# One core, three fused blocks: fixed places for the linear attention's products, an earlier load of the input, and a last column block that is gated and stored by pairs

## The chip, the cores and the metric

The kernel runs on one core of a Trainium2 chip. The metric is the device time of one execution in microseconds (us), and the time of a kernel is the median of its runs. TensorE is written PE here, as in the profile (PEld is its weight load), VectorE DVE, ScalarE ACT, GpSimd POOL, and SyncE, which issues most loads, SP.

## The reference, cut to what matters

Three blocks follow one another on an input of 1024 positions by 1024 features, all in float32. The change touches the first half of block one and the last step of block three.

Block one, first half:

```
h = rmsnorm(x) * norm_mix_g
z = h @ w_in                      # q, k, v, g, a_f, a_b, su, sv
o_f = gla(q, k, v, log_a_f), o_b = the same from right to left, strict
  per chunk of 64 positions: b = cumsum(log_a)
  scores = (q exp(b - b_mid)) @ (k exp(b_mid - b))^T, masked
  state  = exp(b_last) * state + (k exp(b_last - b))^T @ v
  o      = scores @ v + (q exp(b)) @ state
o_gla = rmsnorm_per_head(o_f + o_b) * silu(g)
o_sgu = gelu(su) * (w_s @ rmsnorm(gelu(sv)) + b_s)
x = x + [o_gla, o_sgu] @ w_out
```

Block three, last step:

```
gate = sigmoid(rms_norm(h) @ w_pg);  pe = p @ w_pp
h = h + gate * pe
out = rms_norm(h) * final_g
```

## The kernel before, in words

Every product with a weight matrix is done in three passes: the weights and the activations are each split into a high and a low float32r part, and high by high, high by low and low by high are added in one bank of PSUM (`three`, `mms`). Weights come in units of 256 columns (one unit is one matrix of 1024 rows by 256 columns, 1 MB; some are smaller). A unit passes through four hands: SP loads it (`sp_unit`, one of 3 raw buffers), ACT makes the high part (`act_unit`, L311, one of 2 buffers, after PE has finished the unit two before), DVE makes the low part by a subtraction (`dve_unit`, L320), and PE multiplies (`pe_unit` waits for both parts). Each engine's program calls its own function once a turn; the first turn handles two units (three for SP), so that ACT and DVE are one unit ahead of PE and SP two.

The order of the work is written out by hand, one program for each engine; the same generator code is run on every engine, so that step s of a round has the same meaning everywhere. Each engine runs its instructions in that order, and semaphores tie them together. A `fence` waits for everything of the stage before.

Start: POOL makes an identity and zeroes four 128 by 128 tiles; SP loads 24 small parameter vectors into them (`sp_setup`) and four lambda vectors; PE transposes the four tiles and DVE copies them to `PC`, whose columns are scales and biases; DVE and ACT work out lambda. Then all engines pass the fence "setup", and SP loads x in 8 tiles of 512 KB. ACT squares a tile and sums it (L484), DVE and POOL make the reciprocal root, DVE scales (L562), PE transposes (L359), ACT and DVE split the transposed tile into high and low (L523, L531). The 1024 positions are handled in two halves of 4 tiles. ACT splits the first two weight units after the first half's transposed tiles (`between`), and DVE does its part there too. Then PE does the product for the gates ("a", half 0), the transposes of half 1, and the product "a" of half 1.

Linear attention (`rounds`): 40 pieces of the projection `z = h @ w_in` are called fills. One fill is 48 products of 256 columns or 24 of 512 columns, some 5.7 us of PE. There are ten units (`FILL`: qk0, v0, v1, qk1, g0, g1, sv0, sv1, su0, su1) of four fills each, here called F0 to F39. The attention has four rounds n (head pair 0 and 1, each in both directions) of 11 steps. In round n `back` does the attention of n and `front` prepares the gates of n+1. On PE: step 0 scores of n (64 small products) and the gates' product of n+1 (`la`); steps 1 to 4 the chunk products `kv`, each in two banks of the ring PB of four; steps 6 to 9 the outputs `go`; step 7 a transpose (`kdT`). On DVE: step 1 masks the scores (L1045), steps 2 to 5 read `kv` and run the state forward (L1058, 15 dependent instructions), step 2 also the cumulative sums of n+1 (L952, L954, L961 or L963, L966), steps 3 and 4 the gated q and k (L973, L978, L979), steps 6 and 7 two more of that kind (L982, L987), steps 7 to 10 read `go`. In round 2, `out` for head pair 0 is added: ACT squares (step 0), DVE the mean (step 1, L582), DVE the scaling (step 2, L593), PE four transposes `goT` (step 3, L359), DVE the gating (step 4, L1100). The fills are spread over the steps by `weave`: 8, 4, 4 and 6 of them over the 11 steps of rounds 0, 1, 2 and 3, which puts them after steps 0, 1, 2, 4, 5, 7, 8, 9 in round 0, after steps 0, 3, 6, 9 in rounds 1 and 2, and after steps 0, 2, 4, 5, 7, 9 in round 3. ACT and DVE handle a new unit at the first fill of the unit before it. The last ten fills stand in the tail after round 3.

End (`pe_final` and its partners): for each of four blocks n of 256 columns, PE does `pg` (gate, unit of 1 MB, four pieces of 48 products), then `pp` (embedding, 256 KB, four pieces); ACT takes the sigmoid of a `pg` piece, DVE multiplies by the `pp` piece (L3782), POOL adds to X3 (L3795). After block 3, ACT squares the 8 tiles (L484), DVE and POOL make the reciprocal roots of each half of 4 tiles (L492, L497), DVE scales the tiles (L1583), and SP stores each tile when it is scaled.

## Time and profile before

| | |
|---|---|
| median of 3 runs | 3949.09 us (3943.42 to 3951.37) |
| the profiled execution's own time | 3947.51 us |
| its span, first to last instruction | 3945.6 us |
| PE busy | 3713.4 us, 94% of the span |
| DVE, ACT, POOL busy | 2167.5, 1653.1, 520.3 us |
| PE's share of the chain that ended last | 78% |
| mean granted TensorE clock | 0.973 |

The span is the traced stretch, and the 1.9 us between it and the execution's own time lie around it. "Granted clock" is the share of full TensorE speed that the chip allowed. A timeline row gives start, duration, engine, line, operation, what is written from what, the count, and in brackets the idle time of that engine before it with what ended it. PE bounds the kernel for most of its length, so a microsecond is worth something where PE stands idle or slow, and at both ends of the span, where PE has nothing to do.

### The profile page before, as it was taken

Reading aid. Unit: us, or ns where it says so; the run is one execution under the profiler, and the core shown is the slowest. Engines: PE = TensorE matmul, PEld = TensorE weight load, DVE = VectorE, ACT = ScalarE, POOL = GpSimd, SP = SyncE. Lnnn points to the kernel's source line nnn. Section 1 sums busy time; section 2 is a strip of 40 time slices with the busy share of each in tenths; the row PEclk is TensorE's granted clock in tenths of the full one; section 3 lists DMA queues with packets and bytes.
Section 4 is the critical chain, followed back from the end, with each engine's and each line's share of the span. In section 5 each row is a group of like instructions: output and inputs, shape, how many; then the busy total and the mean of one; then the engine's idle time right before and its main releaser. Section 6 shows DMA issues by size and latency. Waiting matters only on the chain.

```text
span 3945.6 us, 48879 instructions
## 1 busy us (share of the span) xinstructions
PE 3713.4 (94%) x20470; PEld 3102.4 (79%) x20470; DVE 2167.5 (55%) x2859; ACT 1653.1 (42%) x2267; POOL 520.3 (13%) x437
## 2 busy tenths in 40 slices
PE   6979999999999899989999998989999999989998
PEld 5758988877787677777777777978877778778998
DVE  4343344334446566645665655358888877853332
ACT  4322232121113555646776674144555545542132
POOL 0000010010001243510000000012222221210001
PEclk9989999999999899999999999999999999999999
DMA  3101211111111111010111114121111111143111
GB/s 95 33 11 50 75 59 54 43 51 46 43 54 55 43 33 43 12 49 24 33 35 27 35 48 163 49 75 43 43 43 38 49 48 38 38 183 132 44 44 59
DMA packets 196399, 211.32 MB, mean 54 GB/s; under 512 B 7943, under 2 KB 171732, under 8 KB 196180
## 3 DMA queue, kind: packets, MB, share of 16 engines
q1 hardware_dynamic: 191572, 191.42, 15.3%
q10 hardware_dynamic: 4608, 16.78, 1.1%
q8 instruction: 162, 2.65, 0.3%
q14 instruction: 57, 0.47, 0.0%
HBM read 174.62 MB, written 33.55 MB: 53 GB/s over the span
## 4 chain that ended last, share of the span: by engine, by line
PE 78%; DVE 9%; ACT 6%; issue 4%; DMA 1%; POOL 1%; SPq 0%; DVEq 0%; ACTq 0%; POOLq 0%
PE pd L211 66%; PE pq L211 9%; PE pd L359 2%; PE pq L359 1%; ACT t L311 1%; DVE t L320 1%; DVE t L2989 1%; ACT t L2586 1%; DVE t L3426 1%; ACT t L523 1%; DVE t L2981 0%; DVE t L1923 0%; DVE t L1495 0%; DVE t L3411 0%; DVE t L531 0%
## 5 line engine op out<-in xcount | busy, mean ns | idle before, releaser
L211 PE MATMUL pd<-t 128*128 128x512 f32 (+2 forms) x15920 | 3080.9, 354 | 41.6 <-DVE t L1495 10.1
L211 PEld LDWEIGHTS pd<-t 128*128 128x128 f32 x15920 | 2556.5, 191 | 513.0 <-issue 90.2
L211 PE MATMUL pq<-t 128*128 128x128 f32 (+5 forms) x3222 | 542.8, 331 | 83.6 <-DVE t L3465 21.5
L211 PEld LDWEIGHTS pq<-t 128*128 128x128 f32 (+2 forms) x3222 | 391.6, 182 | 184.4 <-issue 47.3
L311 ACT ACTIVATE t<-t 128x2048 fp32r<-128x2048 f32 (+2 forms) x150 | 244.9, 1633 | 677.9 <-PE pd L211 634.0
L320 DVE TENSOR_TENSOR t<-t 128x2048 fp32r<-128x2048 f32 (+2 forms) x150 | 297.3, 1983 | 287.8 <-ACT t L311 287.4
L1495 DVE TENSOR_TENSOR t<-pd,t 128x512 f32<-128x512 f32 x256 | 171.2, 689 | 115.7 <-PE pd L211 115.7
L1486 DVE TENSOR_TENSOR t<-t 128x512 fp32r<-128x512 f32 x64 | 45.8, 719 | 261.3 <-POOL t L1474 261.3
L3378 POOL TENSOR_TENSOR t<-t 128x512 f32<-128x512 f32 x56 | 89.8, 1603 | 616.8 <-ACT t L3322 608.9
L2989 DVE SCALAR_TENSOR_TENSOR t<-t 128x1024 f32<-128x1024 f32 x120 | 169.6, 1413 | 0.5
L2981 DVE SCALAR_TENSOR_TENSOR t<-t 128x1024 f32<-128x1024 f32 x120 | 166.2, 1385 | 1.7
L2709 DVE COPY t<-pd 128x512 f32<-128x512 f32 x64 | 44.3, 691 | 217.6 <-PE pd L359 217.6
L359 PE MATMUL pd<-t 128*128 128x128 f32 x800 | 119.8, 294 | 42.5 <-DVE t L562 18.6
L359 PEld LDWEIGHTS pd<-t 128*128 128x128 f32 x800 | 101.1, 152 | 65.2 <-issue 20.9
L2586 ACT ACTIVATE t<-t 128x1024 f32<-128x1024 f32 x128 | 145.8, 1142 | 13.8 <-DVE t L2663 13.8
L2658 DVE CUSTOM_DVE_ANT_0 t<-pq,t 128x1024 f32<-128x1024 f32 x128 | 151.2, 1219 | 0.0
L3322 ACT ACTIVATE t<-t 128x1024 f32<-128x1024 f32 x56 | 59.4, 1062 | 215.4 <-DVE t L3413 215.4
L1474 POOL TENSOR_TENSOR t<-t 128x512 f32<-128x512 f32 x64 | 68.2, 1067 | 613.1 <-ACT t L1424 613.1
L1424 ACT ACTIVATE t<-pd 128x512 f32<-128x512 f32 x64 | 38.3, 598 | 244.9 <-PE pd L211 244.9
L3426 DVE COPY_PREDICATED t<-t,pq 128x512 f32<-128x512 int32 x128 | 94.7, 743 | 70.1 <-PE pq L211 69.7
L1591 POOL TENSOR_TENSOR t<-t 128x2 f32<-128x2 f32 x8 | 10.4, 1303 | 917.5 <-DVE t L2826 857.1
L713 DVE TENSOR_TENSOR t<-pd,t 128x512 f32<-128x512 f32 x48 | 33.2, 691 | 176.5 <-PE pd L211 176.5
(295 smaller groups left out, 2830.5 us busy)
## 6 DMA issues: line engine op xcount, KB each, us to landing
t<-in_w_in_dram SPq DMA_DIRECT2D x97, 512.0 KB, 4.3
t<-in_w_mlp_dram SPq DMA_DIRECT2D x32, 1024.0 KB, 5.3
t<-in_w_out_dram SPq DMA_DIRECT2D x20, 1024.0 KB, 5.1
t<-in_w_in_dram SPq DMA_DIRECT2D x16, 1024.0 KB, 5.2
t<-in_x_dram SPq DMA_DIRECT2D x16, 512.0 KB, 6.6
x_scratch<-t SPq DMA_DIRECT2D x16, 512.0 KB, 2.6
ym_scratch<-t SPq DMA_DIRECT2D x16, 512.0 KB, 2.6
t<-x_scratch SPq DMA_DIRECT2D x16, 512.0 KB, 20.0
```

What stands on the lines that cost most here:

```text
L211: ins = e.matmul(out, l, r, start=(first and j == 0), stop=(last and j == n - 1), skip_group_check=True)
L311: e.activation(WH[i % 2][:, 0:z], WR[i % 3][:, 0:z], ACT.Copy).then_inc(*at.inc("wh", "wh", i))
L320: e.tensor_tensor(WL[i % 3][:, 0:z], WR[i % 3][:, 0:z], WH[i % 2][:, 0:z].bitcast(F32), SUB).then_inc(*at.inc("wl", "wl", i))
L359: ins = e.transpose(b[:, j * 128:(j + 1) * 128], s, ident[:, :])
L1474: e.tensor_tensor(q[:, :], r[:, :], r[:, :], MUL).then_inc(*at.inc("pool", "q", j, m, th, free=("r", j, m, th)))
L1495: e.tensor_tensor(X1[:, tt, half(nh)], PD.of("down", j, tt, nh)[:, :], X1[:, tt, half(nh)], ADD).then_inc(*at.inc("dve", "xadd", j, tt, nh ...
L2586: e.activation(s[:, r, :], s[:, r, :], ACT.Exp, bias=x[:, 2 + r:3 + r], accum_out=x[:, 4 + r:5 + r]).then_inc(*at.inc("act", "sexp", n))
L2658: e.tensor_tensor_reduce(out=s[:, r, :], in0=PQt[r][:, :], in1=bias[:, 896 - 128 * tt:896 - 128 * tt + 1024], scale=2.0 ** -(h + 1), scala ...
L2981: e.scalar_tensor_tensor(a[:, :], p[:, k:k + S], taps(k, g), a[:, :], MUL, ADD).then_inc(*at.inc("dve", "ctaps", g))
L2989: e.scalar_tensor_tensor(a[:, :], p[:, k:k + S], taps(k, g), a[:, :], MUL, ADD).then_inc(*at.inc("dve", "ctaps", g))
L3378: e.tensor_tensor(v4(z[:, :], w_)[:, :, 0, :], v4(k[:, :], w_)[:, :, 0, :], v4(dd[:, :], w_)[:, :, 0, :], MUL).then_inc(*at.inc("pool", "h ...
L3426: e.copy_predicated(At[:, th * 4:th * 4 + 4, :], bc(Mi[:, l:l + 1, :], [128, 4, 128]), four(PB.of("lv", h, l, th))).then_inc(*at.inc("dve" ...
```

## The change

Four edits, all in the order of work; no product is added or left out.

1. Start. SP's first instructions are the loads of x tiles 0 to 3, then weight unit 0, then x tiles 4 to 7, then the small vectors of tiles 1 to 3 and the lambda vectors. The ten small vectors of tile 0 are loaded from ACT's own queue. The fence "setup" is gone on all engines. PE transposes only tile 0 before x; the other three, and lambda, come after the product "a" of half 1. X0, XN0 and the parameter tiles have memory of their own, side by side.
2. Weight units one by one: the first turn of each engine handles one unit, and one more call stands in `act_norm`, `dve_norm` and twice in `sp_program`. ACT and DVE split unit 0 between the squares of the two halves.
3. Rounds: the fills have fixed places (`FILLS`), 7, 5, 5 and 5 in rounds 0 to 3; DVE handles the next unit at the third fill of a unit, not at the first (but for qk0); the steps of `out` on DVE and PE move from 1, 2, 3, 4 to 2, 4, 5, 6.
4. End. In block 3, `pp` comes before `pg` and writes into PB; after each `pg` piece ACT takes the sigmoid, DVE multiplies and adds to X3 itself, ACT squares the two tiles of the piece into SBUF, DVE and POOL make their reciprocal roots, and DVE scales them one piece later.

```diff
     def act_unit(e):
-        n = turn("act")
-        for i in ([0, 1] if n == 0 else [n + 1]):
-            if i < len(units):
+        i = turn("act")
+        if i < len(units):
...
+    def act_setup(e):
+        e.wait_ge(*at["PR0", 0])
+        for j, (name, ap) in enumerate(COLS[0]):
+            r = col[name]
+            e.dma(PRc[0][r:r + ap.shape[0], :], ap, "col_in", 0, j)
...
     def pe_setup(e):
         e.wait_ge(*at["const"])
+        PB.put(2, ("col", 0))
+        pe_col(e, 0, PB.of("col", 0))
+
+    def pe_setup_rest(e):
+        for i in range(1, 4):
+            pe_col(e, i, e.take(PB, "col", i))
...
     def act_norm(e, X, v, ready, gname, between=lambda e: None):
-        for th in range(2):
-            act_squares(e, X, v, th, ready)
+        act_squares(e, X, v, 0, ready)
+        between(e)
+        act_squares(e, X, v, 1, ready)
...
             for j in range(4):
                 if late:
                     dve_fill_out(e, *late)
-                if j == 0:
+                if j == (0 if name == "qk0" else 2):
                     dve_unit(e)
...
+    FILLS = [(0, 2, 3, 4, 6, 8, 9), (0, 2, 3, 4, 8), (0, 2, 3, 4, 5), (0, 2, 3, 4, 7)]
...
-        for n, pieces in enumerate((8, 4, 4, 6)):
-            weave((round_steps(e, n, front, back, out, more), STEPS), (islice(fill, pieces), pieces))
+        for n, fills in enumerate(FILLS):
+            for s, _ in enumerate(round_steps(e, n, front, back, out, more)):
+                if s in fills:
+                    next(fill)
...
     def dve_out(e, pt, s):
-        if s == 1:
+        if s == 2:
             dve_heads_mean(e, 16, 128, vq if pt == 0 else Sg[:, :, :], 1e-6, "gla", pt)
-        if s == 2:
+        if s == 4:
             dve_heads_scale(e, Of, 16, 128, "gla", pt)
-        if s == 4:
+        if s == 6:
...
     def pe_out(e, pt, s):
-        if s == 3:
+        if s == 5:
...
     def pe_final(e):
         for n in range(4):
+            if n == 3:
+                pe_embedded(e, n)
             u = pe_unit(e, A["w_pg_3"][0], [(n * 256, 256)])
...
+            if n < 3:
+                pe_embedded(e, n)
...
     def act_final(e):
...
+                if n == 3:
+                    for tt in (2 * t4, 2 * t4 + 1):
+                        e.wait_ge(*at["padd_all"])
+                        e.wait_ge(*at["padd", 3, t4])
+                        e.wait_ge(*at.last("act"))
+                        e.activation(stage3[5 + tt % 3][:, :], X3[:, tt, :], ACT.Square,
+                                     accum_out=ss[:, 16 + tt:17 + tt]).then_inc(*at.inc("act", "fss", tt))
...
     def dve_final(e):
...
             for t4 in range(4):
+                gated(n, t4)
+                if n == 3:
+                    o = X3[:, 2 * t4:2 * t4 + 2, 768:1024]
+                    e.tensor_tensor(o, o, two(gtr.of("gt", 3, t4)[:, :]), ADD).then_inc(
+                        *at.inc("dve", "padd", 3, t4, free=("gt", 3, t4)))
+                    if t4 == 0:
+                        e.wait_ge(*at["fg3"])
+                    else:
+                        scaled(t4 - 1)
+                    e.tensor_scalar(st[:, sl], ss[:, sl], 1.0 / 1024, 1e-6, MUL, ADD).then_inc(
+                        *at.inc("dve", "fms", t4))
+        scaled(3)
...
     def sp_program(e):
+        sp_load_x(e, X0, x_in, "x0", tts=range(4))
+        sp_unit(e)
+        sp_load_x(e, X0, x_in, "x0", tts=range(4, NT))
         sp_setup(e)
-        ended("setup", *own)
-        fence(e, "setup")
-        sp_load_x(e, X0, x_in, "x0")
         ended("norm", *own)
+        sp_unit(e)
         sp_unit(e)
```

## Rows read from the trace of the kernel before

**Rows 1.** The page: the span, and the shares of the chain by engine.

```profile
span 3945.6 us, 48879 instructions
...
PE 78%; DVE 9%; ACT 6%; issue 4%; DMA 1%; POOL 1%; SPq 0%; DVEq 0%; ACTq 0%; POOLq 0%
```

**Rows 2.** Timeline, 0 to 57 us: start, duration, engine, line, operation [idle before].

```profile
16.14 3.98 SPq L138 DMA_DIRECT2D t<-in_x_dram  x8
19.67 1.03 ACT L484 ACTIVATE pq<-t 128x1024 f32<-128x1024 f32 x1 [4.10 <-DMA t<-in_x_dram]
...
29.54 6.43 PE L359 MATMUL pd<-t 128*128 128x128 f32 x32 [18.64 <-DVE t L562]
...
30.66 0.69 ACT L523 ACTIVATE t<-pd,t 128x512 fp32r<-128x512 f32 x1 [0.37 <-PE pd L359]
...
37.52 1.41 DVE L531 SCALAR_TENSOR_TENSOR t<-pd,t 128x512 fp32r<-128x512 f32 x2
...
39.50 3.42 DVE L320 TENSOR_TENSOR t<-t 128x1024 fp32r<-128x1024 f32 x2
...
40.82 7.87 PE L211 MATMUL pd<-t 128*128 128x512 f32 x24 [4.86 <-DVE t L320]
...
56.56 12.30 PE L211 MATMUL pd<-t 128*128 128x512 f32 x48
```

**Rows 3.** Windows at the start: busy time of each engine, granted clock, DMA share, GB/s.

```profile
26.00:28.00 2.00, 0.00 (x0) 0.00 (x0) 1.35 (x3) 1.81 (x5) 0.62 (x1) 1.00 1.01 415
...
41.00:49.00 8.00, 8.00 (x29) 6.40 (x30) 1.92 (x1) 0.00 (x0) 0.00 (x0) 0.72 0.00 0
```

**Rows 4.** PE's waits, 68 to 420 us: total us, times, longest.

```profile
PE pq L211 <- DVE t L1045: 9.0, 3, 4.4
PE pq L211 <- DVE t L1058: 8.7, 4, 3.7
PE pq L359 <- DVE t L1058: 8.5, 2, 8.0
PE pq L359 <- DVE t L593: 1.6, 1, 1.6
```

**Rows 5.** Windows: rounds 0 to 2, and round 3.

```profile
115.00:303.00 188.00, 161.77 (x1202) 125.60 (x1203) 82.97 (x112) 57.95 (x64) 2.90 (x1) 0.89 0.07 20
303.00:353.00 50.00, 50.00 (x455) 44.71 (x454) 15.30 (x26) 6.92 (x10) 0.00 (x0) 1.00 0.16 51
```

**Rows 6.** Timeline, rounds 1 and 2.

```profile
183.99 5.74 PE L211 MATMUL pd<-t 128*128 128x512 f32 x24
...
244.32 2.29 DVE L320 TENSOR_TENSOR t<-t 128x2048 fp32r<-128x2048 f32 x1 [13.60 <-ACT t L311]
...
246.53 2.84 DVE L1045 TENSOR_TENSOR t<-pq,t 64x512 f32<-64x512 f32 x4
...
259.04 2.29 DVE L593 TENSOR_TENSOR t<-t 128x2048 f32<-128x2048 f32 x1
...
278.12 7.06 PE L211 MATMUL pd<-t 128*128 128x512 f32 x24
```

**Rows 7.** Groups by line, 115 to 303 us: count, busy us, mean ns, idle before.

```profile
L1058 DVE SCALAR_TENSOR_TENSOR t<-t,pq 128x128 f32<-128x128 f32 x45 | 15.6, 347 | 10.1 <-PE pq L211 8.9
...
L978 DVE TENSOR_TENSOR t<-t 128x1024 f32<-128x1024 f32 x3 | 3.7, 1218 | 0.0
```

**Rows 8.** Timeline, the end.

```profile
3921.31 0.60 ACT L3768 ACTIVATE t<-pd 128x512 f32<-128x512 f32 x1 [5.16 <-PE pd L211]
...
3926.92 0.69 DVE L3782 TENSOR_TENSOR t<-pd,t 128x512 f32<-128x512 f32 x1 [0.72 <-PE pd L211]
3927.18 1.03 ACT L484 ACTIVATE pq<-t 128x1024 f32<-128x1024 f32 x1
...
3935.95 1.01 POOL L497 TENSOR_TENSOR t<-t 128x4 f32<-128x4 f32 x1 [5.07 <-DVE t L492]
3936.99 4.87 DVE L1583 SCALAR_TENSOR_TENSOR t<-t 128x1024 f32<-128x1024 f32 x4 [1.12 <-POOL t L497]
```

More of the change, by code:

```diff
@@ L399, in pc @@
         return PC[:, c:c + 1]
+    x_in = A["x"][0]
     ph = ExitStack()
+    X0 = sbt(ph, [128, NT, 1024])
+    XN0 = [sbt(ph, [128, 1024]) for _ in range(8)]
     PRc = [sbt(ph, [128, 128]) for _ in COLS]
@@ L567, in dve_norm @@
             scaled(tt)
+        between(e)
         dve_rstd(e, v, 1)
@@ L720, in units_only @@
             turns(e)
-    x_in = A["x"][0]
-    ph = ExitStack()
-    X0 = sbt(ph, [128, NT, 1024])
-    XN0 = [sbt(ph, [128, 1024]) for _ in range(8)]
-    ph.close()
     ph = ExitStack()
@@ L3769, in act_final, with gated, scaled @@
                     *at.inc("act", "gt", n, t4, free=("pg", n, t4)))
+                if n == 3:
[5 more added lines that the diff above has]
+                                     accum_out=ss[:, 16 + tt:17 + tt]).then_inc(*at.inc("act", "fss", tt))
             act_unit(e)
-        for th in range(2):
-            act_squares(e, X3, "f3", th, lambda tt: ("padd", 3, tt // 2))
     def dve_final(e):
+        def gated(n, t4):
+            gt = gtr.of("gt", n, t4)
+            e.wait_ge(*at["pp", n, t4])
+            e.wait_ge(*at["gt", n, t4])
+            e.tensor_tensor(gt[:, :], embedded(n, t4)[:, :], gt[:, :], MUL).then_inc(
+                *at.inc("dve", "gp", n, t4, free=("pp", n, t4)))
+        def scaled(p):
+            for tt in (2 * p, 2 * p + 1):
+                e.wait_ge(*at["frstd", p])
+                e.scalar_tensor_tensor(X3[:, tt, :], X3[:, tt, :], st[:, 16 + tt:17 + tt], fg3[:, :], MUL,
+                                       MUL).then_inc(*at.inc("dve", "rms", "f3", tt))
         for n in range(4):
@@ L3796, in pool_final @@
                     *at.inc("pool", "padd", n, t4, free=("gt", n, t4)))
-        pool_rstd(e, "f3", 0)
-        pool_rstd(e, "f3", 1)
+        at.now("pool", "padd_all")
+        for p in range(4):
+            sl = slice(16 + 2 * p, 18 + 2 * p)
+            e.wait_ge(*at["fms", p])
+            e.tensor_tensor(st[:, sl], st[:, sl], nhalf[:, 0:2], ALU.pow).then_inc(*at.inc("pool", "frstd", p))
     def pe_program(e):
         pe_setup(e)
-        ended("setup", "pe")
-        fence(e, "setup")
         pe_stage_gla(e)
@@ L3820, in act_program @@
         act_setup(e)
-        ended("setup", *own)
-        fence(e, "setup")
         act_norm(e, X0, 0, lambda tt: ("x0", tt), "g_mix", between=act_unit)
@@ L3849, in dve_program @@
         own = DVE_OWN
-        dve_setup(e)
-        ended("setup", *own)
-        fence(e, "setup")
+        dve_col(e, 0)
         dve_norm(e, X0, [t[:, :] for t in XN0], 0, lambda tt: ("x0", tt), "g_mix", between=dve_unit)
@@ L3879, in pool_program @@
         pool_setup(e)
-        ended("setup", "pool")
-        fence(e, "setup")
         pool_norm(e, 0)
@@ L3910, in sp_program @@
         own = ["wr0", "wr1", "wr2"] + [f"sp{i}" for i in range(RING["sp"])]
+        sp_load_x(e, X0, x_in, "x0", tts=range(4))
+        sp_unit(e)
+        sp_load_x(e, X0, x_in, "x0", tts=range(4, NT))
         sp_setup(e)
-        ended("setup", *own)
-        fence(e, "setup")
-        sp_load_x(e, X0, x_in, "x0")
         ended("norm", *own)
+        sp_unit(e)
         sp_unit(e)
```

137 lines of the change are left out of this document (68 added, 69 removed).

## The prediction, written before the changed kernel ran

> **What bounds the kernel now.** I read the page first: PE carries 78% of the chain that ended last [rows 1], so anything off PE counts only where PE stands idle. I then read the timeline of the first 57 us, PE's waits and the windows of the attention rounds, and the timeline of the last 25 us, because these are the three places that the change touches. The reader is to see three kinds of lost time.
>
> At the start PE does nothing of use until 29.5 us [rows 2]. The loads of x are issued only at 16.14, behind the small vectors and the fence; the first square runs at 19.67, which is 3.5 us after the first issue. Later PE stands 4.9 us in front of the product "a", until DVE has made the low parts of the first two units (39.50 for 3.42 us); that product then takes 7.87 us, at a granted clock of 0.72 [rows 2, 3].
>
> In rounds 0 to 2 PE waits 9.0 + 8.7 + 8.5 = 26.2 us for DVE [rows 4], exactly what the window 115 to 303 lacks (188.00 − 161.77), and its mean clock there is 0.89. In round 3 there is neither idle time nor a clock under 1.00 [rows 5]. So round 3 shows what an undisturbed round looks like. The masks of the scores (L1045) come late because DVE stands in front of L320, which waits for ACT, which waits for PE to finish a unit: 13.60 us of idle DVE, then 2.29 us of L320, and only then the masks at 246.53 [rows 6].
>
> At the end the last product is over at 3926.9, when DVE takes it up, and the last scaling at 3936.99 + 4.87 = 3941.9, which leaves 15 us with PE at rest [rows 8].
>
> **The change, part by part.**
>
> **Start.** SP has nothing to wait for, so the first load of x can go at about 0.8 us (my estimate: SP's first vector load went at 1.9 behind POOL's zeroing). That moves x by 16.1 − 0.8 = 15.3 us earlier. Unit 0 (512 KB) now stands in the queue between x tiles 3 and 4. At the 415 GB/s of the loads of x [rows 3] that is 1.3 us; its rows are shorter, so I take 1.8. ACT also does unit 0's split, half an L311, about 1 us, between the squares. Part of both overlaps, and I take 1.1 us in all: the first split of a transposed tile (L523), before at 30.66, comes at 30.66 − 15.3 + 1.1 = 16.5 us, a shift of 14.2. From there the sequence is the same down to the end of the transposes (29.54 + 6.43 = 35.97, becoming 21.8) and the last low part (37.52 + 1.41 = 38.93, becoming 24.7). Now nothing stands between them and "a", since unit 0 was split before: "a" follows right behind the transposes. With the same 7.87 us it ends at 21.8 + 7.9 = 29.7, before at 48.69: 19.0 us earlier. With the full clock it would be bounded by the last low part, 24.7 plus about one eighth of 5.7, which is 25.4; that end would give 23 us, and a product that waits for unit 0's low part would give 14.2. I take 19.5. Unit 1's split by ACT and DVE (about 1.9 and 2.3 us) lies beside "a". What its loads are queued behind: SP issues 15 vector and lambda loads first, some 5 us of issuing, until about 10; it must land by 22.5 when ACT comes to it. x ends at about 15 and 1 MB more takes 2.5 to 4 us, so it lands near 20. That cover is thin: 2 us. The three parameter transposes move behind the second "a", on PE's path, for 3 short transposes: 0.5 us. DVE's copies and lambda, and ACT's exponential with perhaps one more table load, lie beside fills F0 to F3. Start: 19.5 − 0.5 = 19 us.
>
> The ten vector loads on ACT's queue: what waits behind them is the first square, which cannot run before x lands at about 4.4 us; and PE's first transposes, DVE's copy and then all of the norm on DVE wait for them to land. DVE has no other work before 10 us. Cost between 0 and 3 us; I take 0, since an issue takes some 0.3 us each. The Trainium skill (DMA: Bandwidth & Descriptors, Issuing engines are not separate DMA queues) says that loads started by ScalarE and SyncE run on the same 16 DMA engines and interleave. By it ACT's queue gives the vectors no lane of its own, and they share the engines with x in the busiest stretch: with its rule the cost tends to the upper end, 3 us of the sum, and without it to none. The trace of before has no two queues at work at once in this stretch, so it cannot tell.
>
> **Rounds.** I replayed the three rounds from the durations of the timeline. Moving DVE's unit to the third fill removes L320, and with it the wait for ACT, from in front of the masks. In rounds 0 and 1 a whole fill (5.74 us [rows 6]) now covers the masks and their step: 2.84 us from the end of the scores. The next read of `kv` has four dependent instructions at 0.35, 1.5 us in all [rows 7], and the fills after steps 2, 3 and 4 cover the cumulative sums and the gated q and k. I find no wait of PE left there, 0 to 2 us. Before, rounds 0 and 1 had 9.1 us of idle time.
>
> Round 2 is denser, and there one wait stays. DVE has, from the end of the logarithm on ACT: cumulative sums 5.4, mean 2.5, second `kv` read 1.5, about 1.4 waiting for the exponential behind ACT's gate work, gated q 1.2, L320 2.3, third `kv` read 1.5, gated k and its partner 2.4, scaling 2.3 [rows 6, 7]: 20.5 us. PE has from the same point only the rest of F21 and then F22 and F23, some 16 us. So `goT`, now in step 5, waits about 4.8 us (bounds 0 and 9). Before, the same round cost 17 us of waits; the 8.0 us wait for L1058 in front of `goT` [rows 4] becomes this one.
>
> The clock: a fill takes 7.06 us behind these waits and 5.74 elsewhere [rows 6], and the window's 0.89 over 161.77 busy us is at most 17.8 us lost [rows 5]. A part of the low clock falls on idle time, so I take 12. That is 12 us of slow products to 26.2 of idle, and the 4.8 us that stay bring in proportion 2.2. In sum rounds 0 to 2 give (26.2 + 12) − (4.8 + 2.2) = 31.2.
>
> The tail has one wait for the second head scaling, 1.6 us [rows 4], which came from an L320 in front of it; the unit is now done one step earlier: 1.6 saved. Fills, `kv`, `go` and transposes are the same in number, and each is drained by ACT one fill later, within the four banks of the ring. In round 2 ACT's copy of F20 waits for the mean, now one step later, by which time PE has filled four banks with F20 to F23; that copy is done about 7 us before F24 wants the bank. Rounds and tail: 33 us (bounds 16 and 40).
>
> **End.** PE's amount of work is the same, so its last product still ends at E = 3926.9 less the shifts. `pp` of block 3 comes first; the weights of its `pg` can be loaded only when `pg` of block 2 is done, and then 1 MB has to land (some 5 us), be split by ACT (1.9) and DVE (2.3): some 10 us, against 11.5 us of `pp` 2 and `pp` 3. It fits by about 1.5 us. After E: sigmoid 0.60, multiply 0.69, add on DVE about 0.69, two squares 2 × 1.2, mean 0.17, POOL's power 1.01, two scalings at 4.87/4 = 1.22, that is 2.4 [rows 8], and seven handovers of about 0.06: 8.4 us, against 15.0 before. The other three pairs are done under the product, one each 5.8 us, for which DVE needs 4 us. What POOL did in 1.3 us, DVE now does in 0.7, and the stores of the last tile take as long as before. End: 6.6 us (bounds 4 and 8).
>
> The sum is 19 + 33 + 6.6 = 58.6 less 1 us for what I may have missed at the joints, 57.6. The profiled execution took 3947.5 us in itself, 1.9 more than its span, and lies 1.6 us under the median of the runs: 3947.5 − 57.6 = 3889.9, and by the median 3891.5. I say 3891.
>
> **The rivals.** First, DVE stays the bound of the rounds: the waits only move. For it speaks that DVE is nearly full in the middle of round 2 and that my 4.8 us there is a difference of two long chains. Against it, DVE is busy for only 82.97 of 188 us [rows 5]. Half of the gain of the rounds would go, 16 us, and the time would be 3907. Second, the start is bounded by loads: with the vectors on ACT's queue landing late (3 us), or unit 1 landing late so that the second "a" and F0 wait (up to 6 us), the start gives 10 instead of 19: 3900. For it speaks the thin cover of 2 us, against it that x at 415 GB/s leaves the queue early. Third, on the other side: DVE's low part, now made two fills before its use and not four, comes too late, and PE waits at the first fill of each unit. Nine units from v1 on would have to wait 57.6 / 9 = 6.4 us each to bring the time back to 3949, and 8 us each would give 3963. That needs DVE to be more than two fills (11.5 us) behind in each round; the replay has it at most 5 us behind, once. Fourth, the clock stays low in spite of fewer waits: 12 us are not given back, 3903.
>
> **How the numbers follow.** The forecast, with all three places within their bounds near my values, has 0.72. The first rival 0.10, the second 0.08, the fourth 0.06, the third 0.03; 0.01 is that nothing measurable changes. The range reaches up to the first rival, 3907, and down to where the start gives 23, the rounds 37 and the end 7.5, which is 3881. A measurement of this kernel tells about 0.2% (8 us) from no change: faster 0.96, same 0.01, slower 0.03.
>
> **What would show it.** The first x load in the first 1.5 us, and the product "a" right behind the transposes, ending near 30 us. PE's waits for L1045 gone. One wait of PE at `goT`, for L593 rather than L1058, of about 5 us; no others over 1 us in rounds 0 and 1. A mean clock of about 0.97 or more over the rounds. From the last product to the last scaling 8 to 9 us. The prediction is wrong if L320 shows up as what PE waits for in the rounds, or if the stages between 410 and 3820 us of before take another length by more than 3 us.

## The result, and the profile after: 3885.4 us

The changed kernel takes 3885.4 us in the median of four runs (3881.2 to 3886.4), against 3949.6 us for the kernel before on the same chip (four runs, 3943.4 to 3951.4). The ratio is 0.9838, with a 95% interval of 0.9821 to 0.9855. That is 64.2 us by the medians and 61.3 us by the two profiled executions (3947.5 and 3886.2). I had said 3891. The working below goes by the profiled executions.

The page of the kernel after, which answers to [rows 1]. PE's share of the chain that ended last rose from 78% to 81%, while "issue" lost one point and DVE one.

```profile
span 3884.3 us, 48877 instructions
...
PE 81%; DVE 8%; ACT 6%; issue 3%; DMA 1%; POOL 1%; ACTq 0%; SPq 0%; DVEq 0%; POOLq 0%
```

Where the time went is read from one list of marks: moments that are the same piece of work in both kernels, each as far from the start of the span as the timeline shows it.

| mark | before | after | shift |
|---|---|---|---|
| first load of x issued | 16.14 | 0.80 | −15.3 |
| product "a", first half, ends | 48.69 | 29.18 | −19.5 |
| round 0 begins (its first scores) | 111.15 | 92.69 | −18.5 |
| the four rounds end | 352.28 | 302.19 | −50.1 |
| tail of the stage ends | 404.11 | 352.24 | −51.9 |
| a mark early in the next block | 568.69 | 515.26 | −53.4 |
| last product ends | 3926.88 | 3873.07 | −53.8 |
| last scaling ends | 3941.86 | 3881.07 | −60.8 |
| span | 3945.6 | 3884.3 | −61.3 |

So the start gave 18.5 us, the rounds 31.6, the tail 1.8 and the end 7.0, with 0.5 more behind the last scaling. The 1.9 us between the tail and the last product lie in stages that the change doesn't touch. Most of them are a matter of the clock, of which the section on the hardware says more.

**The start.** Timeline of the kernel after; it answers to [rows 2]. Columns: start, duration, engine, line, operation, and in brackets the idle time before it with what ended it.

```profile
0.80 1.81 SPq L138 DMA_DIRECT2D t<-in_x_dram  x4
...
4.41 0.31 ACTq L138 DMA_DIRECT2D t<-in_ssm_norm_g_dram  x1
...
5.75 0.23 ACTq L138 DMA_DIRECT2D t<-in_subln_g_dram  x1
6.01 1.28 ACT L503 ACT_TABLE_LOAD   x1 [6.01 <-DMA t<-in_norm_mlp_g_dram]
...
7.30 1.03 ACT L503 ACTIVATE pq<-t 128x1024 f32<-128x1024 f32 x1
...
10.60 0.45 PE L439 MATMUL pq<-t 128*128 128x128 f32 x1 [10.60 <-DMA t<-in_subln_g_dram]
...
16.41 4.41 PE L356 MATMUL pd<-t 128*128 128x128 f32 x24 [5.36 <-DVE t L582]
...
17.80 1.28 ACT L542 ACTIVATE t<-pd,t 128x512 fp32r<-128x512 f32 x2
...
23.46 5.72 PE L211 MATMUL pd<-t 128*128 128x512 f32 x24 [0.86 <-ACT t L542]
...
31.19 1.31 PE L356 MATMUL pq<-t 128*128 128x128 f32 x8 [1.13 <-DVE t L550]
33.41 1.97 PE L356 MATMUL pq<-t 128*128 128x128 f32 x8 [0.91 <-DVE t L550]
...
37.71 6.89 PE L211 MATMUL pd<-t 128*128 128x512 f32 x24
```

The reader is to see three things. The product "a" stands right behind the transposes (0.86 us of idle time in place of 4.86), and it takes 5.72 us in place of 7.87. ACT's ninth vector load goes out at 4.41 and its tenth only at 5.75, and the first square follows at 7.30. And two equal sets of eight transposes take 1.31 and 1.97 us, one after the other: the clock fell between them.

**The rounds.** All of PE's waits between 45 and 370 us of the kernel after (total us, times, longest), where before there were 27.8 us in ten waits [rows 4]:

```profile
PE pq L356 <- DVE t L614: 4.4, 1, 4.4
```

Windows of the kernel after, over rounds 0 to 2, as in [rows 5]: length, busy time of PE, PE's weight loads, DVE, ACT and POOL, then granted clock, DMA share and GB/s.

```profile
110.00:300.00 190.00, 185.56 (x1489) 148.64 (x1488) 85.30 (x124) 55.65 (x63) 2.90 (x1) 0.98 0.10 31
```

PE lacks 4.4 us of the 190, and the clock is 0.98 where it was 0.89. Timeline of the kernel after, around the masks of round 1 and the one wait of round 2, to be held against [rows 6]:

```profile
153.49 2.85 DVE L1058 TENSOR_TENSOR t<-pq,t 64x512 f32<-64x512 f32 x4 [6.11 <-PE pq L211]
...
156.04 7.36 PE L211 MATMUL pd<-t 128*128 128x512 f32 x24
...
234.15 3.15 PE L356 MATMUL pq<-t 128*128 128x128 f32 x16 [4.44 <-DVE t L614]
...
236.96 6.52 PE L211 MATMUL pd<-t 128*128 128x256 f32 x48
```

The masks (here L1058, before L1045) now wait for the scores and for nothing else, and a fill of 24 products runs beside them. In round 2 the transposes of `goT` wait 4.44 us for the head scaling (L614, before L593), and 16 of them then take 3.15 us.

**The end.** Timeline of the kernel after, as in [rows 8]: one chain of single steps, each of half or a quarter of the former size.

```profile
3873.11 0.60 ACT L3796 ACTIVATE t<-pd 128x512 f32<-128x512 f32 x1 [1.27 <-PE pd L211]
3873.80 0.69 DVE L3812 TENSOR_TENSOR t<-pq,t 128x512 f32<-128x512 f32 x1 [1.77 <-ACT t L3796]
3874.53 0.69 DVE L3830 TENSOR_TENSOR t<-t 128x512 f32<-128x512 f32 x1
...
3875.26 1.06 ACT L3803 ACTIVATE t<-t 128x1024 f32<-128x1024 f32 x1 [1.55 <-DVE t L3830]
...
3877.86 0.69 POOL L3853 TENSOR_TENSOR t<-t 128x2 f32<-128x2 f32 x1 [5.05 <-DVE t L3838]
3878.59 2.48 DVE L3818 SCALAR_TENSOR_TENSOR t<-t 128x1024 f32<-128x1024 f32 x2 [0.81 <-POOL t L3853]
```

From the last product (3873.09) to the last scaling (3881.07) it is 8.0 us, before 15.0.

### The profile page after: what moved, and what is told of

Same layout as the page of the kernel before. It is cut to its first block, busy times and chain, and to the rows that moved or that the text cites. A ratio compares the mean times of both kernels' runs of the same rounds, so it can differ in the third digit from the quotient of the medians.

```text
span 3884.3 us, 48877 instructions
## 1 busy us (share of the span) xinstructions
PE 3697.9 (95%) x20470; PEld 3091.1 (80%) x20470; DVE 2169.5 (56%) x2865; ACT 1652.5 (43%) x2267; POOL 519.8 (13%) x435
## 4 chain that ended last, share of the span: by engine, by line
PE 81%; DVE 8%; ACT 6%; issue 3%; DMA 1%; POOL 1%; ACTq 0%; SPq 0%; DVEq 0%; POOLq 0%
PE pd L211 68%; PE pq L211 10%; PE pd L356 2%; PE pq L356 1%; ACT t L310 1%; DVE t L318 1%; ACT t L2607 1%; DVE t L3010 1%; ACT t L542 1%; DVE t L3447 1%; DVE t L3002 0%; DVE t L1944 0%; DVE t L1516 0%; DVE t L550 0%; DVE t L1629 0%
## 5 line engine op out<-in xcount | busy, mean ns | idle before, releaser
L318 DVE TENSOR_TENSOR t<-t 128x2048 fp32r<-128x2048 f32 (+2 forms) x150 | 296.1, 1974 | 214.1 <-ACT t L310 213.7
```

What stands on the lines that cost most here:

```text
L318: e.tensor_tensor(WL[i % 3][:, 0:z], WR[i % 3][:, 0:z], WH[i % 2][:, 0:z].bitcast(F32), SUB).then_inc(*at.inc("wl", "wl", i))
```

## The experiments

The edits are against the kernel after. Those with a median were run three to five rounds beside the kernel before, whose medians in the three sets were 3946.6, 3944.1 and 3944.3, so 3.0 to 5.5 us under the 3949.6 above. Those with one profiled execution are held against the profiled 3886.2 of the kernel after. Times of whole executions therefore carry some 3 to 5 us that no edit made, and a second list gives the stretches between the marks in each trace (us). "Before round 0" is the mark of its first scores, "rounds" and "tail" are the lengths up to the next two marks, and "rest" is what lies between the tail and the last product, which only old_end and pg_first touch, at its very end.

| kernel | before round 0 | rounds | tail | rest |
|---|---|---|---|---|
| before | 111.2 | 241.1 | 51.8 | 3522.8 |
| after | 92.7 | 209.5 | 50.1 | 3520.8 |
| late_x | 106.3 | 209.5 | 50.1 | 3520.8 |
| split_late | 98.0 | 209.5 | 50.1 | 3520.6 |
| old_rounds | 90.9 | 240.6 | 51.8 | 3522.8 |
| old_end | 90.4 | 211.0 | 50.1 | 3521.9 |
| pg_first | 90.5 | 209.5 | 50.1 | 3518.7 |
| weave_places | 90.7 | 227.5 | 50.0 | 3520.1 |
| unit_first | 92.6 | 211.6 | 51.9 | 3520.2 |
| steps_early | 92.1 | 214.1 | 50.1 | 3523.9 |
| unit_last | 90.6 | 208.8 | 50.1 | 3519.6 |
| two_fills | 92.0 | 201.6 | 50.1 | 3518.9 |
| ring10_two_fills | 91.9 | 203.2 | 50.1 | 3520.6 |
| cols_sp_two_fills | 93.3 | 201.7 | 50.1 | 3522.3 |

A stretch that an edit doesn't touch shows what comes without it: up to 2.3 us at the start and up to 3.1 us in the rest. The rounds carry some 1.6 us of the same kind: two_fills and ring10_two_fills have the same rounds, yet they take 201.6 and 203.2 us, since one fill of round 1 took 5.7 us in the first and 7.3 in the second.

### Each place undone by itself

**late_x.** The vectors and lambda are set up first, with the fence, and x is loaded behind them; unit 0 is still split between the squares.

```
         own = ["wr0", "wr1", "wr2"] + [f"sp{i}" for i in range(RING["sp"])]
+        sp_setup(e)
+        ended("setup", *own)
+        fence(e, "setup")
         sp_load_x(e, X0, x_in, "x0", tts=range(4))
         sp_unit(e)
         sp_load_x(e, X0, x_in, "x0", tts=range(4, NT))
-        sp_setup(e)
...
```

> The changed kernel, with only one thing put back: the small vectors, lambda and the fence come first, and x is loaded behind them as before; unit 0 is still split between the squares. My theory: x early is worth 16.1 - 0.8 = 15.3 us at the first load, but in the changed kernel ScalarE's first square ran 6.5 us after the first load and not 3.5 us (ten vector loads and a table load stand in front of it), so putting x back costs 15.3 - 3.0 = 12.3 us: about 3898 against 3885.4, and the product 'a' follows the transposes directly as in the changed kernel. The rest of the start's 18.5 us (about 6) belongs to the split of unit 0 ahead of the transposes. Rival, that the early load alone makes the gain and the place of the split is worth nothing: 3885.4 + 18.5 = 3904.

Measured: 3898.9 us (3897.1 to 3899.9), ratio 0.9883 (0.9868 to 0.9897), so 13.5 us over the kernel after. Timeline of this kernel:

```profile
16.36 1.75 SPq L138 DMA_DIRECT2D t<-in_x_dram  x4
...
38.31 5.71 PE L211 MATMUL pd<-t 128*128 128x512 f32 x24 [0.86 <-ACT t L523]
```

"a" ends at 44.0: 4.7 us earlier than before, which is what the early split of unit 0 gives alone, and 14.8 us later than in the kernel after, which is what the early x gives there. By the start of round 0 the early x is worth 13.6. My theory had 12.3, its rival 18.5.

**split_late.** The other half of the start: x stays early, units 0 and 1 are both split behind the first half of the norm.

```
         act_squares(e, X, v, 0, ready)
-        between(e)
         act_squares(e, X, v, 1, ready)
...
             if th == 0:
                 between(e)
+                between(e)
```

> The changed kernel, but units 0 and 1 are both split after the first half's transposed tiles, as before; x is loaded as early as in the changed kernel. Theory: the product 'a' waits for unit 0's low part again, some 3.2 us, and the clock falls in the wait (7.9 us for the product and not 5.7): its end comes 3 to 5.5 us later than 29.15, and so does the rest. Rival, x early is all that counts: within 1 us, since ScalarE's squares end 1 us earlier.

Measured: 3891.3 us in one run, 5.1 over. Timeline of this kernel: the wait for the low parts of unit 0 is back, and so is the slow product behind it.

```profile
26.41 3.42 DVE L318 TENSOR_TENSOR t<-t 128x1024 fp32r<-128x1024 f32 x2
27.73 7.56 PE L211 MATMUL pd<-t 128*128 128x512 f32 x24 [5.14 <-DVE t L318]
```

"a" ends at 35.3, which is 6.1 later than in the kernel after, and round 0 begins 5.3 later. With late_x this settles the start: at round 0, 13.6 us from the loads and 5.3 from the split, against 18.5 together.

**old_rounds.** Places of the fills, DVE's unit and the steps of the outputs as before.

```
-        for n, fills in enumerate(FILLS):
-            for s, _ in enumerate(round_steps(e, n, front, back, out, more)):
-                if s in fills:
-                    next(fill)
+        for n, pieces in enumerate((8, 4, 4, 6)):
+            weave((round_steps(e, n, front, back, out, more), STEPS), (islice(fill, pieces), pieces))
...
-                if j == (0 if name == "qk0" else 2):
+                if j == 0:
...
```

> The changed kernel with the rounds of before: fills spread by the weave, VectorE's unit at the first fill, the head steps at 1, 2, 3, 4. Theory, the parts add up: the markers of the two traces give 31.6 us for the rounds and 1.8 us for the tail behind them, so 3885.4 + 33.4 = 3918.8, with waits of TensorE of 27.8 us as in the kernel before. Rival, the earlier start or the moved memory changed the rounds too: less than 28 or more than 38 us.

Measured: 3920.1 us (3918.2 to 3922.0), ratio 0.9938 (0.9921 to 0.9954), 34.7 over. PE's waits of this kernel, 45 to 372 us:

```profile
PE pq L211 <- DVE t L1058: 9.0, 3, 4.5
PE pq L356 <- DVE t L1071: 8.5, 2, 8.0
```

With 11.0 us for L1071 at the reads of `kv` and 1.6 for L614 these are 30.1 us of waits. By the marks, rounds and tail take 32.9 us more than in the kernel after, and are within 0.5 us of the kernel before. 30.1 − 4.4 = 25.7 us of it are idle time, the other 7.2 a slower clock (0.95 from 45 to 372 us, where the kernel after has 0.99).

**old_end.** The last columns, their gating and the last norm as before.

```
         for n in range(4):
-            if n == 3:
-                pe_embedded(e, n)
             u = pe_unit(e, A["w_pg_3"][0], [(n * 256, 256)])
...
-        for p in range(4):
-            sl = slice(16 + 2 * p, 18 + 2 * p)
-            e.wait_ge(*at["fms", p])
-            e.tensor_tensor(st[:, sl], st[:, sl], nhalf[:, 0:2], ALU.pow).then_inc(*at.inc("pool", "frstd", p))
+        pool_rstd(e, "f3", 0)
+        pool_rstd(e, "f3", 1)
...
```

> The changed kernel with the last step of block three as before. Theory: from TensorE's last product to the last scaling it is 15.0 us again, not 8.0, so 3885.4 + 7.3 = 3892.7, within 1 us in the trace. Rival, that the end's gain is taken back by the stores (which now are issued while x3 is still being worked on): less than 4 us.

Measured: 3892.7 us (3890.7 to 3893.7), ratio 0.9867 (0.9852 to 0.9882), 7.3 over. The timeline of this kernel shows the old end again:

```profile
3883.48 4.87 DVE L1604 SCALAR_TENSOR_TENSOR t<-t 128x1024 f32<-128x1024 f32 x4 [1.12 <-POOL t L516]
```

### Which part of an edit does it

**pg_first.** The pairs stay, but in block 3 `pg` is multiplied before `pp`.

```
         for n in range(4):
-            if n == 3:
-                pe_embedded(e, n)
             u = pe_unit(e, A["w_pg_3"][0], [(n * 256, 256)])
...
-            if n < 3:
-                pe_embedded(e, n)
+            pe_embedded(e, n)
```

> The changed kernel, but in block 3 the gate product comes before the embedding product again; the work by pairs stays. Theory: ScalarE's next sigmoid is queued behind the squares of the pair before, and those wait for an embedding piece that now comes last, so the four pairs run one after another from 4.3 us before the last product, each some 4.5 us: the last scaling comes 16.4 us after the last product, 8.4 us more than in the changed kernel, and 1.4 us worse than before. Rival, the work by pairs alone makes the gain and the order is of no matter: within 1.5 us of the changed kernel's 8.0 us.

Measured: 3890.1 us in one run. From the last product (3868.7) to the last scaling it is 16.3 us, in place of 8.0:

```profile
3877.02 0.58 ACT L3793 ACTIVATE t<-pd 128x512 f32<-128x512 f32 x1
...
3882.49 2.48 DVE L3815 SCALAR_TENSOR_TENSOR t<-t 128x1024 f32<-128x1024 f32 x2 [0.81 <-POOL t L3850]
```

The sigmoids are ACT's, and they stand in its order behind the squares of the pair before. When `pg` comes first, a pair takes 4.37 us on ACT and DVE while PE ends one in 1.5, so the pairs pile up behind the last product (the last sigmoid runs 8.3 us after it). When `pp` comes first, PE needs 5.8 us a pair and the two engines keep up. The total rose by only 3.9 us, because in this run the last product was already over 4.3 us earlier (3868.7 in place of 3873.1), 2.2 of it before round 0, where the mean clock from 16 to 60 us was 1.00 and not 0.92, and 2.1 in the stages between the tail and block 3's last columns, where the code is the same. So the order is worth the 8.3 us by which that stretch is longer. Without it the pairs bring nothing: 16.3 us is more than the 15.0 of before.

**weave_places, unit_first, steps_early.** The three edits of the rounds, each undone alone: the places of the fills (the first part of old_rounds' diff), DVE's unit (`if j == 0`, its second part), and the steps of the outputs:

```
     def dve_out(e, pt, s):
-        if s == 2:
+        if s == 1:
             dve_heads_mean(e, 16, 128, vq if pt == 0 else Sg[:, :, :], 1e-6, "gla", pt)
-        if s == 4:
+        if s == 2:
             dve_heads_scale(e, Of, 16, 128, "gla", pt)
...
```

> The changed kernel with the fills spread by the weave again (8, 4, 4, 6 over the steps of rounds 0 to 3); VectorE's unit at the third fill and the later head steps are kept. Theory A, the places carry the gain: with four fills in round 1, the third chunk product waits for the read of the first (1.2 us) and the first output product stands right behind the fourth chunk product with no fill between, some 6 us of wait; round 2 the same plus the head scaling (some 15 us); with the clock some 22 us more than the changed kernel. Theory B, which the prediction gave for rounds 0 and 1: the gain comes from VectorE's unit leaving the masks' way, and then the places alone are worth less than 8 us.

> The changed kernel with only VectorE's unit put back to the first fill of a unit. Theory A (places carry it): the masks wait behind L318 in rounds 0 and 2 only, since in round 1 the first fill of a unit now stands at step 2; 2.4 us of wait in round 0 and 4.4 us in round 2, the latter taken from the wait at the head transposes: 3 to 5 us more than the changed kernel. Theory B: the waits for L1045 of before (9.0 us, with their clock some 13) all come back.

> The changed kernel with only the head steps of the output put back to 1, 2, 3, 4 (transposes in step 3). Theory: the mean moves into idle time of VectorE, but the transposes then come 12 us earlier and wait 4 to 5.5 us for the scaling and for the read of the second chunk product, and everything behind the scaling is 2.3 us later: 0 to 3 us more than the changed kernel. Rival, the later steps are what makes room in round 2: over 6 us more.

Measured, in one run each: weave_places 3901.4 us (15.2 over), unit_first 3889.4 (3.2 over), steps_early 3893.3 (7.1 over). PE's waits, 45 to 372 us, of weave_places:

```profile
PE pq L211 <- DVE t L1071: 11.1, 5, 5.3
PE pq L356 <- DVE t L614: 6.3, 1, 6.3
```

of unit_first:

```profile
PE pq L211 <- DVE t L1058: 5.2, 2, 2.8
PE pq L356 <- DVE t L614: 1.6, 1, 1.6
```

and of steps_early:

```profile
PE pq L356 <- DVE t L1071: 8.2, 2, 5.5
```

What follows is read from the marks, since the totals hold up to 3.1 us from outside the edits. In rounds and tail together, the places carry 17.9 us, the unit 4.0 and the steps 4.6, each good to some 1.6.

The places are less than the 22 of my theory and far more than the 8 of its rival. They are what covers the reads of `kv` (L1071: 11.1 us of waits without them, none with them).

The unit does clear the masks: their waits are 9.0 in old_rounds, and none in weave_places, where the unit is already moved. But with the places right, putting it back costs only 2.1 us in the rounds: it brings 5.2 us of waits at the masks and takes the whole 4.4 at `goT` of round 2 away, since L318 then no longer stands in front of that head scaling. The 1.6 us for L614 are another wait, in the tail, and the tail is 1.9 us longer by it. Timeline of unit_first, `goT` of round 2 and of the tail:

```profile
237.85 1.91 PE L356 MATMUL pq<-t 128*128 128x128 f32 x16
...
323.49 1.97 PE L356 MATMUL pq<-t 128*128 128x128 f32 x16 [1.63 <-DVE t L614]
```

For the steps neither side is borne out: 4.6 us in the rounds lie between my theory (0 to 3) and the rival (over 6), and the other 2.5 of the 7.1 come from stretches that the edit doesn't touch. The timeline of steps_early shows the two waits:

```profile
218.85 2.28 DVE L614 TENSOR_TENSOR t<-t 128x2048 f32<-128x2048 f32 x1
221.05 1.49 DVE L1071 SCALAR_TENSOR_TENSOR t<-t,pq 128x128 f32<-128x128 f32 x4
...
222.69 1.94 PE L356 MATMUL pq<-t 128*128 128x128 f32 x8 [5.52 <-DVE t L1071]
223.59 2.28 DVE L318 TENSOR_TENSOR t<-t 128x2048 fp32r<-128x2048 f32 x1
...
227.34 1.97 PE L356 MATMUL pq<-t 128*128 128x128 f32 x8 [2.71 <-DVE t L1071]
```

`goT` writes into the banks that the reads of `kv` use. Two steps earlier it needs those banks while DVE has not yet read them, and the second of them stands behind L318. But its operand is late there too: the scaling L614 ends at 221.13 and the read of the first bank at 222.54, so only the last 1.4 of the 5.52 us are the bank's, and with the 2.71 of the second bank that makes 4.1 of the 8.2. The rest is the wait for the scaling, some 4 us with either place of the steps.

The three parts undone singly add to 26.5 us in rounds and tail, undone together to 32.9. So some 6 us are lost only when more than one of them is undone, and that figure is rough, since one fill at the lower clock adds 1.6 to any of these lengths.

**unit_last.** DVE's unit one fill later still, for my third rival (a low part that comes too late).

```
-                if j == (0 if name == "qk0" else 2):
+                if j == (0 if name == "qk0" else 3):
```

> The changed kernel with VectorE's unit at the fourth fill of a unit, one fill before TensorE needs it. The third rival of the prediction expects waits of TensorE for L318 at the first fill of some units, and more time. My theory expects none: VectorE is never a whole fill behind when it gets there; in round 2 the unit moves behind the head scaling, which then comes 2.3 us earlier, so the wait of 4.4 us falls to about 2.1 and the rounds take 2 to 3 us less than in the changed kernel.

Measured: 3882.2 us in one run, 4.0 under the profiled kernel after. Its PE waits are 2.2 (L614) and 2.1 (L1071), and none for L318: even with one fill of lead the low part is never late. The wait for L614 fell to 2.2 as forecast, but a wait of 2.1 for a bank of `goT` took its place, so the rounds are only 0.7 us shorter and not 2 to 3 (less than what one fill more or less at the lower clock makes). The other 3.3 of the 4.0 are not the edit's: 2.1 stand before round 0, where the mean clock from 16 to 60 us was 1.00 in this run and 0.92 in the kernel after, and 1.2 in the rest.

### The wait that stayed, and the queue at the start

**two_fills.** In round 2 the fourth and fifth fill both stand in front of `goT`.

```
-    FILLS = [(0, 2, 3, 4, 6, 8, 9), (0, 2, 3, 4, 8), (0, 2, 3, 4, 5), (0, 2, 3, 4, 7)]
+    FILLS = [(0, 2, 3, 4, 6, 8, 9), (0, 2, 3, 4, 8), (0, 2, 3, 4, 4), (0, 2, 3, 4, 7)]
...
-                if s in fills:
+                for _ in range(fills.count(s)):
                     next(fill)
```

> The changed kernel with the fifth fill of round 2 placed after step 4 and not after step 5, so that two fills stand in front of the head transposes. Theory: the one wait that is left in the rounds (4.4 us for L614) goes, and with it the slow clock behind it (transposes 3.15 us and not 1.9, the fill 6.5 and not 6.0): 6 us less than the changed kernel, about 3879. Rival, the wait moves to the first output product, which waits for the gating that follows the transposes (2.7 us on VectorE): at most 3 us less.

Measured: 3875.4 us (3874.7 to 3876.7), ratio to the kernel before 0.9824 (0.9807 to 0.9840). PE has no wait at all from 45 to 372 us. Timeline and window of this kernel:

```profile
232.98 1.91 PE L356 MATMUL pq<-t 128*128 128x128 f32 x16
...
249.51 6.02 PE L211 MATMUL pd<-t 128*128 128x256 f32 x48
```

```profile
110.00:300.00 190.00, 190.00 (x1554) 153.03 (x1554) 89.97 (x126) 57.52 (x65) 3.57 (x2) 1.00 0.10 31
```

The fill at 249.51 began at 258.07 in the kernel after: 8.6 us, of which 2.3 stood before round 2 began and 6.2 come from round 2. That is the wait of 4.4, the 16 transposes, 1.2 us shorter (1.91 in place of 3.15), and a fill, 0.5 us shorter (6.02 in place of 6.52). It is the best version that I ran. Of the 10 us between its median and that of the kernel after, 6.2 are shown to be the edit's; the two ratios to the kernel before lie 0.0014 apart, some 5.5 us, though their intervals overlap.

**ring10_two_fills.** On top of it, ten landing semaphores for ACT's queue in place of eight (`RING = {"sp": 16, "act": 10}`), so that no load waits for one to come free.

> two_fills, and in addition ten landing semaphores for ScalarE's loads and not eight, so that the ninth and tenth vector load no longer wait for the first two to land. Theory: the first square comes 1.3 us earlier (6.0 and not 7.3), the last square and everything behind it some 1 us: 3874.4 against 3875.4 of two_fills. Rival, the start is bounded by the landing of x and not by ScalarE's queue: no change at the product 'a' (start at 23.5).

Measured: 3878.5 us (3874.2 to 3879.3), not faster. The first square moved from 7.43 to 6.65, 0.8 us and not the 1.3 that I expected, and the last one only from 16.87 to 16.62. Timeline of this kernel:

```profile
6.65 1.03 ACT L503 ACTIVATE pq<-t 128x1024 f32<-128x1024 f32 x1
...
16.62 1.03 ACT L503 ACTIVATE pq<-t 128x1024 f32<-128x1024 f32 x1 [0.35 <-DMA t<-in_x_dram]
...
23.35 3.00 PE L211 MATMUL pd<-t 128*128 128x512 f32 x12 [0.87 <-ACT t L542]
```

Now the last square waits 0.35 us for x. "a" starts at 23.35 against 23.59: the landing of x bounds the start, which was the rival.

**cols_sp_two_fills.** The ten vectors are issued on SP's queue behind the first four tiles of x, in place of ACT's.

```
         sp_load_x(e, X0, x_in, "x0", tts=range(4))
+        e.wait_ge(*at["PR0", 0])
+        for j, (name, ap) in enumerate(COLS[0]):
+            r = col[name]
+            e.dma(PRc[0][r:r + ap.shape[0], :], ap, "col_in", 0, j)
         sp_unit(e)
```

> two_fills, and in addition the ten vectors of tile 0 are loaded by SyncE, behind x tiles 0 to 3 and ahead of unit 0, and not by ScalarE. Theory: ScalarE is free for its table load at once, the first square comes at 4.4 us when x tile 0 has landed, the last at 16.3 and not 17.9, and the product 'a' starts 1.6 us earlier: 3873.8 against 3875.4. Rival: unit 0 and x tiles 4 to 7, now issued 3.3 us later, come too late for ScalarE, and the start is the same or up to 2 us later.

Measured: 3879.5 us (3877.6 to 3880.6), ratio 0.9832 (0.9818 to 0.9845), not faster. Timeline of this kernel:

```profile
4.39 1.03 ACT L502 ACTIVATE pq<-t 128x1024 f32<-128x1024 f32 x1 [2.29 <-DMA t<-in_x_dram]
...
12.05 1.06 ACT L310 ACTIVATE t<-t 128x1024 fp32r<-128x1024 f32 x1 [1.73 <-DMA t<-in_w_in_dram]
...
24.05 2.29 PE L211 MATMUL pd<-t 128*128 128x512 f32 x9 [0.87 <-ACT t L541]
```

The first square runs at 4.39, just as I had forecast for the kernel after. But the ten issues put the later x tiles 3.5 us back on SP's queue (6.79 in place of 3.31), and unit 0 with them, and unit 0's split waits for its load; "a" starts at 24.05 and round 0 at 93.3, against 23.59 and 92.0 in two_fills, which is the rival. So ACT's queue was the better place for the vectors.

## Why the prediction was right, point by point

**Start: 19 forecast, 18.5 measured, and two errors in it that cancelled.** The first load of x at 0.8 and the first split of a transposed tile at 16.5 (measured 17.8) were the frame. ACT's first square came at 7.30 and not at 4.4: ten issues and the table load stand in front of it, and ring10_two_fills shows that the wait for landing semaphores is only 0.8 us of that. From 7.30 on ACT works without a gap until the last square is done at 17.8. But starting sooner would have gained little, since x lands no faster: the last square waits for x until 16.10 in split_late and until 16.62 in ring10_two_fills, and with 1.2 us for that square the first split can't come before 17.3 to 17.8. So my 0 us for the vectors was off by some 0.5 us at most (an estimate from those two runs). The larger error is the landing of x, which I had put at about 15, with 415 GB/s from the window of before. The window of the kernel after shows 356 GB/s, with the DMA engines fully busy (share 1.01):

```profile
4.50:16.00 11.50, 0.45 (x1) 0.18 (x1) 2.94 (x6) 9.52 (x15) 1.02 (x1) 1.00 1.01 356
```

The other error was the 7.87 us that I left to "a". It ran at full speed in 5.72, since PE came to it from transposes with 0.86 us of idle time and not out of 4.86 us. It began at 23.46 for my 21.8, 1.7 us late, and was 2.15 us shorter, which makes its end 29.18 for my 29.7. That the two errors nearly cancelled was luck. From there to round 0 the kernel after takes 1.0 us more than the one before, where I had put 0.5 for the three transposes: the transposes of half 1 ran at a lower clock (1.97 us twice for eight, before 1.31 and 1.77). The first load of unit 1 was issued at 15.37 and not at about 10, but ACT took the unit at 23.22 without a wait, and nothing of PE waits for it.

**Rounds and tail: 33 forecast, 33.4 measured.** The waits for the masks are gone, and one wait stays at `goT` for the head scaling, 4.4 for my 4.8. The clock over the rounds is 0.98. Of the 31.6 us of the rounds 26.2 − 4.4 = 21.8 are idle time, which leaves 9.8 for the clock, just what my terms of 12 and 2.2 gave. old_rounds brings the waits back almost as they were (30.1 us) and costs 32.9 in rounds and tail. What was off is the weight of the reasons. I replayed all three edits together and led with DVE's unit, in front of the masks. Undone alone the unit gives 4.0 us and the places of the fills 17.9, so the cover is worth more than the head start. The later steps of the outputs have no term of their own in the prediction, and they give 4.6.

**Tail.** 1.6 forecast, 1.8 measured; the wait for the second scaling is gone, and unit_first, in which it is back, shows that it is the unit that cleared it.

**End: 6.6 forecast, 7.0 and 0.5 behind it measured.** The chain is 8.0 us for my 8.4. POOL's power is most of the difference: over two columns it takes 0.69 us, where I had kept the 1.01 of four. pg_first shows that the cover under the last products, on which I had spent a sentence, decides the whole gain.

**The joints.** I took off 1 us for what I may have missed. There was nothing, and the stages between the tail and the last product came out 1.9 us shorter, inside the 3 us that I had set as the mark of an error. These 1.9 us and the 1 that I took off are 2.9 of the 3.7 by which the sum of 57.6 falls short of the 61.3 of the traces.

**The rivals.** The first (DVE stays the bound, 3907) and the fourth (the clock stays low, 3903) are refuted by the waits and the window of the kernel after. The second (loads bound the start, 3900) came in neither of its two forms: the norm did not wait for the vectors, and unit 1 was not late. What bounds the start in ring10_two_fills is the landing of x, which costs about 1 us against my 16.5 for the first split, not 9. The rule of the Trainium skill that I weighed there (DMA: Bandwidth & Descriptors, Issuing engines are not separate DMA queues) agrees with this trace, where the tenth vector load took 4.85 us from issue to use (5.75 to 10.60) amid the loads of x; before, with no load of x beside it, it took 1.50 (5.05 to 6.55). The 3 us that I had put beside the rule were not lost, because nobody on the path waited for the vectors: DVE's copy of them ended at 11.38, and the norm began at 12.21, behind the fourth square. The third (low parts too late) is refuted by unit_last.

What stays open: how the 6 us that the three edits of the rounds share are divided among pairs of them. I did not run the pairs. And the three singly undone ones are single runs; their totals are good to some 3 us each, and I read them by the marks. Why the clock differed between kernels in stretches with the same code is not shown either.

## What to carry to other kernels

When a chain of short steps on a second engine must be done before the next product, put a full piece of independent product work beside it, as long as the whole chain; to have the chain start a little sooner was worth much less here (4 us against 18). A step can wait for the buffer it writes as well as for its operand, so look at who last reads the buffer before it is moved forward. And when single runs are compared, compare stretches between marks, since the totals here moved by up to 4 us outside the edits. At the end of a kernel, let the operand that the longest chain needs come first, and check that each pair's chain is shorter than the product it hides under; otherwise splitting in pairs brings nothing.

## What the hardware showed that I had not expected

**The same code at another clock.** From 16 to 60 us, where the code of these kernels is equal, the granted clock was 0.92 in the kernel after, 0.96 in two_fills and 1.00 in pg_first and unit_last. Windows of the kernel after and of pg_first:

```profile
16.00:60.00 44.00, 39.51 (x177) 31.47 (x178) 23.78 (x38) 23.42 (x32) 5.39 (x11) 0.92 0.26 75
```

```profile
16.00:60.00 44.00, 39.77 (x187) 31.72 (x188) 25.75 (x39) 23.31 (x32) 5.39 (x11) 1.00 0.26 74
```

A clock of 1.00 is the upper of the two levels, 2.4 GHz, and 0.92 is a mean with some time at 1.2 GHz in it. The second half of "a", behind transposes with three gaps of about 1 us each, took 5.72 or 5.73 us in five of the kernels (old_rounds, old_end, pg_first, weave_places, unit_last) and 6.55 to 7.12 in most others. And the fill at 156.04 of the kernel after took 7.36 us, though PE had no idle time in front of it: what came before were 68 small products of 64 by 64. The same fill took 7.31 us in ring10_two_fills and 5.74 in two_fills, whose rounds are the same. Outside the change, 35 us of the next block ran at 0.96 in the kernel before and at 1.00 in the kernel after, which is most of the 1.9 us above. In the single runs of pg_first and unit_last 4.3 us and 3.3 of the 4.0 come from stretches that their edits don't touch, which only the marks tell from the edit.

**Landing semaphores that run out stall the issuer.** In this kernel a load waits until the earlier load on its semaphore has landed. The first eight vector loads went out on ACT's queue 0.3 to 0.6 us apart; the ninth at 4.41 and the tenth at 5.75 waited for earlier ones to land, and ACT's first square with them. With ten semaphores the table load began at 5.35 in ring10_two_fills, in place of 6.14 in two_fills.

**Small sizes.** POOL's power took 0.69 us over two columns and 1.01 over four, so half the columns saved a third. The sum of 128x512 took DVE 0.69 us, where POOL had taken 5.52 for four of them, 1.38 each.
